# A hybrid decoder trunk on one core: where the second block's mixer is placed among the expert retrieval of the first

## The chip, the cores and the metric

The kernel runs on one core of a Trainium2 chip. The metric is the device time of one execution in microseconds (us). Engines: PE (TensorE), DVE (VectorE), ACT (ScalarE), POOL (GpSimd) and SP (SyncE, which only issues DMAs here). The 16 DMA engines of the core move everything between HBM and SBUF.

## What is computed

Input x is 256 tokens of 1024 float32 values. Two layers follow, each a mixer and an expert retrieval (PEER), both added to the residual stream, and a final RMSNorm. Cut to its core:

```python
for layer in range(2):
    hn = rms_norm(h, norm1_g[layer])
    proj = hn @ w_in[layer]                      # 1024 -> 2824
    o_a = gdn_mixer(...)        # gated delta rule, 4 heads, with a triangular inverse
    o_b = s5_mixer(...)         # diagonal state space scan, 16 groups x 64 states
    o_c = diff_attn_mixer(...)  # causal differential attention, 4 heads
    h = h + concat([o_a, o_b, o_c]) @ w_out[layer]
    h = h + peer_ffn(rms_norm(h, norm2_g[layer]), ...)

def peer_ffn(x, wq, keys, u_tab, v_tab):         # for each token and each of 8 heads
    # two top-16 of 128 sub-keys, top-16 of their 256 sums: 16 experts of 16384
    gate = softmax(top_s)
    act = gelu(einsum('bthkd,btd->bthk', u_tab[expert], xt))
    return einsum('bthk,bthkd->btd', gate * act, v_tab[expert])
```

Each token needs 8 x 16 rows of u_tab and as many of v_tab, of 4 KB each.

## The kernel before

**Blocks, pairs, slots.** A block is 128 tokens in one layer; there are four, numbered i = 0 to 3 (layer i // 2, token half t = i % 2). PEER of a block takes its 8 heads in 4 pairs, and a pair of heads has 32 slots. In a slot one row of u_tab per partition is gathered (128 x 1024, 0.524 MB), DVE forms its dot product with the token (`dot`, L1699), and one row of v_tab is gathered, which PE later weighs and sums over the partitions (`values`). All 16 pairs, n = 0 to 15, run as one chain of 512 dots. A selection `top(n + 1)` (L1610 to L1683) runs on DVE in small parts among the dots of pair n; it yields the indices of the next pair's gathers.

**The mixer of the next block rides along.** Block 0's mixer runs alone at the start (`first_mixer`). While the four pairs of block b are worked off (128 slots), every engine also works off the mixer of block b + 1, cut in steps. PE, DVE and ACT each have their own generators `mix(i)` and `attention(i)`, which yield the slot at which the next step is due; after slot j of pair n the engine calls `stages.advance(PAIR * (n % 4) + j)`, which runs all steps whose due slot is not above that number. The numbers are written out by hand (34, 36, 38, 44.6, ... 121), and `place(i, slot)` (L111) turns them into slots: as they are for blocks 2 and 3, and by a straight line for block 1, because block 1 has no tables to make (these are slots 1 to 28 of blocks with t = 0) and so can use the slots that these take elsewhere. A due slot sets the order within an engine's program; what is waited for is semaphores alone.

**Steps spoken of here**, by their written number s. DVE: norm1 (the reciprocal of the root, L1424) at 34; log decay at 42 and 44.3; the four S5 parts `ssm(i, j)` (L1375 to L1392) at 44.6, 48.9, 54 and 59; `silu` (L1593) at 51.5 and 53.2; the lower triangle at 62.3; S5 output at 65 and 66.3; GLU at 68.2; masks (L1588) at 59.6 + 3 lv; attention maximum (L1399) at 69.8; attention scales and differences to 75.2; residual (L1518) at 99; second norm (L1521, L1524) at 100; `top(4 * i)` from 109 to 118.1; gates at 121. ACT: the square and root of the second norm (`norm_square`, L2077 and L2079) at 99.5. PE: turning the normed input at 36, the weight fills from 38 on.

**Weights.** A mixer reads 39 chunks of 0.524 MB (`CHUNKS`: u, qkv, z, v, q, k, two halves each, glu, the output projection, PEER's wq), which SP loads into a ring of 4 (`wring`), one each time PE has used one. Block 1's first six chunks are loaded ahead, into v buffers 5 to 10.

**Rings and the order on GpSimd.** Gathers are issued by GpSimd from one in-order program: for each slot j of pair n the u gather (it waits until the dot 7 rows before is done, since `uring` has 7 buffers), then as many v gathers as `v_goal(n, j)` asks for. In pair 0 v starts at slot 11 and takes every second slot, until all 11 buffers of `vring` are asked for. v gather q, counted from 0, waits for these things:

```python
            elif q >= VRING:
                pool.wait_ge(v_used.sem, q - VRING + 1)
            elif q >= FREE_SLOT:                                # FREE_SLOT = 5
                pool.wait_ge(*chunk_done(1, q - FREE_SLOT + 1))
            elif q == 0:
                pool.wait_ge(*chunk_done(0, NC))
```

PE sums the rows of pair n in pair n + 1, four rows at a time, in slots 1, 5, ... 29, once DVE has written their weights (`weights(n)`, after the first dot of pair n + 1).

**ACT within a pair.** In slot 24 ACT makes the softmax of the next pair; in slot 31, ahead of the mixer's steps due there, it waits for the pair's gelu argument from DVE:

```python
                if j == PAIR - 1:
                    act.wait_ge(gelu_arg.sem, n + 1)
                    S.activation(gt, gt, ACT.Tanh, scale=GELU).then_inc(gelu_tanh.sem, 1)
                stages.advance(PAIR * (n % 4) + j)
```

DVE's slot 31 is: dot, `gelu(n)` (which signals the argument), then the mixer's steps due.

Of the kernel before, what the change touches and what calls it, by code (L numbers as in the profile page):

```python
# [110 lines left out]

def place(i, slot):

    return slot if i != 1 else 2 + (slot - 32) * 117.0 / 88.0


class Stages:
# [19 lines left out]
def _build(nc, ctx, x, w_blocks, cols_d, rows_d, keys_d, u_tab, v_tab, cst_d, fin_d, out):  # L137
# [419 lines left out]
    def _(pe):  # L557
# [358 lines left out]
        def mix(i):  # L916
            t, layer = i % 2, i // 2
            yield place(i, 36)
            pe.wait_ge(*hn1_ready(i, 1))
            if i == 1:  # L920
                pe.wait_ge(s0_ready.sem, 5)
            else:
                pe.wait_ge(*sc_ready(i, 0))
            turn_mix((M0, M1))
            yield place(i, 38)
            pe.wait_ge(*trT_ready(i, 1))
            fill(i, "u", 0, M2, True)
            yield place(i, 39)
            pe.wait_ge(*trT_ready(i, 2))
            fill(i, "u", 1, M2, True)  # L930
# [1718 lines left out]
```

## Time and profile before

| | |
|---|---|
| median of 3 runs | 1603.93 us (1601.36 to 1607.55) |
| profiled execution | 1604.18 us, its span 1602.2 us |
| DVE, POOL, PE busy | 1110.2, 987.0, 967.3 us |
| ACT busy | 292.0 us |
| moved by DMA | 628.66 MB, mean 392 GB/s |
| of it by gathers (POOL's queue) | 536.94 MB |
| of it by SP's queue | 90.53 MB |

The span counts from the first to the last instruction. The page cuts it in 40 slices of 40 us; in those from 280 us on the DMA engines move 407 to 420 GB/s, but for three (385, 354 and the last, 307). The times of the four pairs of block 0, by the first dot of each in the trace, are 146.7, 215.8, 305.8 and 392.8 us, and block 1's pairs begin at 489.2 us.

### The profile page before, as it was taken

What the parts mean: (1) busy time and instruction counts of PE and PEld (TensorE: products, weight loads), DVE (VectorE), ACT (ScalarE), POOL (GpSimd) and SP (SyncE); (2) the same over time, 40 slices, a digit from 0 to 9 for tenths busy, and PEclk for the clock granted to TensorE, in tenths of its full rate; (3) what the DMA queues carried; (4) which work ended last, traced back from release to release, by engine and by line L of the source; (5) the groups of instructions that cost most, each with busy time, mean ns of one, the idle gap of its engine ahead of it and who ended that gap; (6) DMA issues with size and microseconds to landing.
All of it is one profiled execution on the core that took longest, in us unless ns stands there. A gap on an engine that the chain in (4) does not pass through costs nothing.

```text
span 1602.2 us, 18901 instructions
## 1 busy us (share of the span) xinstructions
PE 967.3 (60%) x5966; PEld 565.9 (35%) x5966; DVE 1110.2 (69%) x2868; ACT 292.0 (18%) x830; POOL 987.0 (62%) x1031
## 2 busy tenths in 40 slices
PE   9986796865634357887554347977674334333335
PEld 8875674532400036654330024844350000000001
DVE  5948999775657987777466766779557767676440
ACT  5343421411000032332110014314110000000000
POOL 0003656777666676657657775646757777777773
PEclk9998898977866579999776568989886555555567
DMA  9527999999999999999999999999999999999997
GB/s 373 200 91 255 384 371 419 407 419 419 418 420 420 417 385 419 418 419 419 419 419 420 419 420 418 418 416 354 419 420 419 419 419 420 419 419 419 420 418 307
DMA packets 172899, 628.66 MB, mean 392 GB/s; under 512 B 19200, under 2 KB 19200, under 8 KB 172800
## 3 DMA queue, kind: packets, MB, share of 16 engines
q0 software_dynamic: 147456, 536.94, 82.8%
q1 hardware_dynamic: 25344, 90.53, 14.4%
q8 instruction: 47, 0.77, 0.2%
q14 instruction: 52, 0.43, 0.1%
HBM read 626.34 MB, written 1.05 MB: 392 GB/s over the span
## 4 chain that ended last, share of the span: by engine, by line
DMA 28%; DVE 24%; POOL 17%; issue 14%; PE 12%; DVEq 4%; ACT 1%; POOLq 0%; SPq 0%; ACTq 0%
DMA uring<-in_u_tab,small 19%; PE ps L559 12%; DVE uring L1699 10%; POOL uring L2505 7%; POOL vring L2505 6%; DMA vring<-in_v_tab,small 4%; DMA wring<-in_v_tab,small 1%; DMA gd<-in_u_tab,small 1%; POOL gd L2505 1%; POOL wring L2505 1%; DMA uring<-in_v_tab,small 1%; DMA rows<-in_rows 1%; DVE sel L1659 1%; DVE small L1636 1%; DVE sel L1663 1%
## 5 line engine op out<-in xcount | busy, mean ns | idle before, releaser
L1699 DVE CUSTOM_DVE_ANT_0 uring<-uring,ps 128x1024 f32<-128x1024 f32 x462 | 558.3, 1217 | 282.8 <-DMA uring<-in_u_tab,small 262.9
L2505 POOL DMA_INDIRECT uring<-in_u_tab,small x462 | 446.3, 966 | 405.4 <-DVE small L1699 136.6
L559 PE MATMUL ps<-vring,wmat 128*32 128x512 f32 x1748 | 328.3, 874 | 397.4 <-DMA vring<-in_v_tab,small 343.9
L2505 POOL DMA_INDIRECT vring<-in_v_tab,small x437 | 419.9, 961 | 151.1 <-issue 115.6
L559 PEld LDWEIGHTS ps<-vring,wmat 128*32 128x32 f32 x1748 | 58.7, 138 | 587.9 <-DMA vring<-in_v_tab,small 396.4
L559 PE MATMUL ps<-hnT,wring 128*128 128x128 f32 x1200 | 151.5, 283 | 1.7 <-ACT hn L2013 1.2
L559 PEld LDWEIGHTS ps<-hnT,wring 128*128 128x128 f32 x1200 | 142.3, 196 | 25.6 <-issue 20.6
L559 PE MATMUL ps<-wring,hnT 128*128 128x256 f32 x344 | 84.4, 396 | 1.8 <-ACT hnT L2013 1.5
L2495 ACT ACTIVATE small<-small 128x32 f32<-128x32 f32 x16 | 3.7, 230 | 442.5 <-DVEq L1708 442.5
L559 PE MATMUL ps<-gd 128*128 128x128 f32 (+1 forms) x508 | 70.4, 289 | 15.4 <-ACT gd L2013 13.5
L559 PEld LDWEIGHTS ps<-gd 128*128 128x128 f32 x508 | 63.6, 196 | 31.7 <-ACT gd L2013 17.6
L2013 ACT ACTIVATE gd<-ps 128x512 f32<-128x512 f32 (+2 forms) x79 | 43.2, 548 | 165.7 <-PE ps L559 145.4
L559 PEld LDWEIGHTS ps<-wring,hnT 128*128 128x128 f32 x344 | 65.8, 199 | 21.4 <-issue 10.0
L1699 DVE CUSTOM_DVE_ANT_0 gd<-gd,ps 128x1024 f32<-128x1024 f32 x40 | 48.8, 1220 | 33.4 <-DMA gd<-in_u_tab,small 33.2
L559 PE MATMUL ps<-phase_c,wmat 128*32 128x512 f32 x28 | 25.0, 1048 | 43.6 <-DMA vbuf<-in_v_tab,small 43.6
L2288 ACT ACTIVATE small<-small 128x16 f32<-128x16 f32 x32 | 6.6, 209 | 230.1 <-DVE small L1647 229.9
L559 PE MATMUL ps<-kT,wmat 128*32 128x512 f32 x28 | 23.6, 994 | 40.9 <-DMA vring<-in_v_tab,small 34.0
L559 PE MATMUL ps<-wring,wmat 128*32 128x512 f32 x112 | 23.6, 987 | 37.5 <-DMA wring<-in_v_tab,small 30.4
L2505 POOL DMA_INDIRECT gd<-in_u_tab,small x40 | 37.5, 937 | 12.2 <-issue 11.6
L559 PE MATMUL ps<-cst 128*128 128x512 f32 x76 | 41.9, 640 | 2.4 <-ACTq L2051 1.7
L1699 DVE DVE_READ_ACCUMULATOR2_ANT small<- 128x1 f32 x512 | 42.4, 83 | 0.0
L559 PE MATMUL ps<-sa,cz 128*32 128x128 f32 x224 | 31.7, 308 | 4.4 <-DVEq L1393 4.4
(434 smaller groups left out, 1501.7 us busy)
## 6 DMA issues: line engine op xcount, KB each, us to landing
wring<-in_w_blocks SPq DMA_DIRECT2D x120, 512.0 KB, 7.2
vring<-in_w_blocks SPq DMA_DIRECT2D x32, 512.0 KB, 9.4
uring<-in_u_tab,small POOLq DMA_INDIRECT x462, 12.3
vring<-in_v_tab,small POOLq DMA_INDIRECT x437
wring<-in_cols SPq DMA_DIRECT2D x3, 512.0 KB, 6.9
sa<-in_rows SPq DMA_DIRECT2D x3, 512.0 KB, 6.5
h<-in_x SPq DMA_DIRECT2D x2, 512.0 KB, 8.9
keysT<-in_keys SPq DMA_DIRECT2D x2, 512.0 KB, 13.2
```

The lines of the kernel that those rows point to most:

```text
L559: return nc.tensor.matmul(o, a, b, start=start, stop=True, skip_group_check=True)
L1636: V.max_index(tp[:, hd, 0:8], tv[:, hd, 0:8], cand1[:, hd, :])
L1659: V.tensor_tensor(oh.rearrange("p g k n -> p (g k) n"), bc(ab_f[:, pc][:, :, None], [P, 32 * nh, TOPK]), bc(iota[:, None, :], [P, 32 * nh, ...
L1663: V.tensor_tensor(oh, oh, bc(sif[:, pc].rearrange("p (g n) -> p g n", n=TOPK)[:, :, None, :], [P, 2 * nh, TOPK, TOPK]), ALU.mult)
L1699: V.tensor_tensor_reduce(row_, row_, xp, 1.0, 0.0, ALU.mult, ALU.add, dots[:, j:j + 1]).then_inc(dot_done.sem, 1)
L2013: return S.activation(dst, src, ACT.Copy, scale=scale)
L2288: S.activation(gate[:, hd, :], gate[:, hd, :], ACT.Exp, accum_out=gz[:, hd:hd + 1])
L2495: S.activation(gt, gt, ACT.Tanh, scale=GELU).then_inc(gelu_tanh.sem, 1)
L2505: nc.gpsimd.indirect_dma_start(dst, None, table, bass.IndirectOffsetOnAxis(ap=index, axis=0)).then_inc(done.sem, 16)
```

## The change

One line: the straight line by which block 1's written numbers become slots.

```diff
 def place(i, slot):
 
-    return slot if i != 1 else 2 + (slot - 32) * 117.0 / 88.0
+    return slot if i != 1 else 10 + (slot - 32) * 110.0 / 88.0
```

Number 32 maps to slot 10 in place of slot 2, number 120 to slot 120 in place of 119. It holds for PE, DVE and ACT alike; SP's and GpSimd's programs don't call `place`. No instruction and no transfer is added or taken away, and blocks 0, 2 and 3 are placed as before.

## Rows read from the trace of the kernel before

**Rows 1.** The page: busy time of the engines, and landing times of the gathers.

```profile
...
PE 967.3 (60%) x5966; PEld 565.9 (35%) x5966; DVE 1110.2 (69%) x2868; ACT 292.0 (18%) x830; POOL 987.0 (62%) x1031
...
uring<-in_u_tab,small POOLq DMA_INDIRECT x462, 12.3
...
```

**Rows 2.** Stretches of the span: busy us per engine, PE clock, DMA share, GB/s.

```profile
...
138.00:172.00 34.00, 19.47 (x156) 18.33 (x157) 32.13 (x106) 15.95 (x44) 23.18 (x25) 0.80 0.93 335
172.00:200.00 28.00, 17.83 (x101) 14.93 (x101) 26.11 (x64) 10.54 (x28) 15.78 (x16) 0.80 1.00 389
200.00:235.00 35.00, 33.80 (x250) 27.98 (x249) 32.03 (x82) 10.93 (x40) 18.77 (x19) 0.97 0.97 364
235.00:280.00 45.00, 32.80 (x215) 21.47 (x214) 41.91 (x98) 7.93 (x14) 29.41 (x30) 0.89 1.02 418
280.00:305.00 25.00, 22.95 (x138) 12.72 (x137) 19.58 (x44) 10.75 (x32) 17.33 (x19) 1.00 1.01 402
305.00:550.00 245.00, 122.82 (x676) 57.35 (x680) 169.14 (x487) 24.35 (x66) 167.89 (x177) 0.72 1.03 419
...
```

**Rows 3.** Waits of DVE, 305 to 550 us: total us, times, longest.

```profile
...
DVE uring L1699 <- DMA uring<-in_u_tab,small: 59.8, 41, 3.8
...
```

**Rows 4.** DVE in order of time: start, us, instruction, idle before it.

```profile
...
155.85 0.15 DVE L1424 RECIPROCAL small<-small 128x1 f32<-128x1 f32 x1
...
172.36 1.20 DVE L1699 CUSTOM_DVE_ANT_0 uring<-uring,ps 128x1024 f32<-128x1024 f32 x1
...
215.78 1.21 DVE L1699 CUSTOM_DVE_ANT_0 uring<-uring,ps 128x1024 f32<-128x1024 f32 x1
...
```

**Rows 5.** DVE by line, 198 to 216 us: count, busy us and mean ns, idle before.

```profile
...
L1385 DVE TENSOR_TENSOR_SCAN sa<-small,sa 128x128 f32<-128x128 f32 x4 | 1.6, 466 | 0.1
L1593 DVE SCALAR_TENSOR_TENSOR keyT<-keyT,ps 128x512 f32<-128x512 f32 (+1 forms) x2 | 1.1, 553 | 0.1
L1375 DVE TENSOR_TENSOR sa<-sa,phase_c 128x512 f32<-128x512 f32 x1 | 0.7, 693 | 1.1 <-PE ps L559 1.1
...
L1378 DVE TENSOR_TENSOR sa<-sa 128x256 f32<-128x256 f32 x1 | 0.4, 426 | 0.1
...
```

**Rows 6.** DVE in order of time, at the attention's maximum.

```profile
...
282.58 1.29 DVE L1399 TENSOR_REDUCE small<-ps 128x2 f32<-128x512 f32 x2 [2.03 <-PE ps L559]
...
```

**Rows 7.** GpSimd in order of time: v gathers 5, 10 and 11.

```profile
...
175.62 0.98 POOL L2505 DMA_INDIRECT vring<-in_v_tab,small  x1 [0.31 <-issue]
...
201.26 0.94 POOL L2505 DMA_INDIRECT vring<-in_v_tab,small  x1 [0.30 <-issue]
...
223.27 0.94 POOL L2505 DMA_INDIRECT vring<-in_v_tab,small  x1 [0.30 <-issue]
...
```

**Rows 8.** PE in order of time: the turned input, chunks 1 and 2, 7 and 8.

```profile
...
157.24 1.97 PE L562 MATMUL ps<-cst,hn 128*128 128x128 f32 x8 [13.65 <-ACT hn L2013]
159.61 4.63 PE L559 MATMUL ps<-hnT,vring 128*128 128x128 f32 x32 [0.40 <-ACTq L2106]
...
175.48 3.84 PE L559 MATMUL ps<-hnT,wring 128*128 128x128 f32 x32
...
```

**Rows 9.** DMA issues, 150 to 200 us: count, median us to landing.

```profile
...
uring<-in_u_tab,small POOLq DMA_INDIRECT x23, 6.0
...
```

**Rows 10.** DVE in order of time, at block 1's second norm.

```profile
...
385.64 0.16 DVE L1521 RECIPROCAL small<-small 128x1 f32<-128x1 f32 x1 [0.31 <-ACT small L2079]
385.89 1.28 DVE L1524 SCALAR_TENSOR_TENSOR hn<-h,small,sa 128x1024 f32<-128x1024 f32 x1
...
```

**Rows 11.** ACT in order of time, at block 1's second norm.

```profile
...
382.81 1.06 ACT L2077 ACTIVATE hn<-h 128x1024 f32<-128x1024 f32 x1 [39.06 <-DVE h L1518]
...
384.02 1.28 ACT L2079 ACT_TABLE_LOAD   x1
385.31 0.29 ACT L2079 ACTIVATE small<-small 128x1 f32<-128x1 f32 x1
...
```

## The prediction

> **What bounds the kernel now.** I read the slices of the page first, for the course of the transfers, then the stretches of the trace around block 1's mixer, then who waits for whom, then single instructions. The vector engine is busy for 69% of the span, GpSimd for 62% [rows 1]: neither fills it. The bound is what the 16 DMA engines move. From 305 to 550 us they move 419 GB/s without a break [rows 2], and there the dot products (DVE L1699) stand 59.8 us idle waiting for their gathered rows [rows 3]. At 419 GB/s a gather of 0.524 MB takes 1.25 us, and the vector engine needs 1.2 us for a dot; a slot (one dot, one u row, one v row) costs 2.5 us of transfer, more where weights are loaded. So an engine's saving counts only where the DMA engines move less than 419 GB/s.
>
> Around this change they do so here [rows 2]: 172 to 200 us 389 GB/s, which is 28 x 30/419 = 2.0 us lost; 200 to 235 us 364 GB/s, 4.6 us; 235 to 280 us 418 GB/s, 0.1 us; 280 to 305 us 402 GB/s, 1.0 us. From 138 to 172 us 335 GB/s are moved, but this is the start of pair 0, ahead of every step that the change can touch except one reciprocal. What can be won is thus at most 2.0 + 4.6 + 0.1 + 1.0 = 7.7 us, and only as far as the cause of the loss is the mixer's vector work. That the vector engine is the cause is seen in its busy time in these stretches, 26.1 of 28 us and 32.0 of 35 us [rows 2].
>
> **What moves, and when.** A step of block 1 with number s was due at slot 2 + 1.330(s-32) and is due at slot 10 + 1.25(s-32). The first vector step, s = 34, goes from 4.7 to 12.5; s = 54 from 31.3 to 37.5; s = 70 from 52.5 to 57.5; s = 100 from 92.4 to 95; the last, s = 121, from 120.3 to 121.3. Nothing is added or removed: no instruction, no byte. Block 1 still hands over within pair 3, and the selection for pair 4 ends at s = 118.1, slot 117.6 for 116.5; GpSimd wants those indices when dot 122 (of 128) is done, so that costs nothing as long as the lead of 4 slots isn't used up. Blocks 2 and 3 keep their slots. Whatever block 1 gains or loses by slot 128 carries to the end unchanged.
>
> **Pair 0, vector engine.** norm1's reciprocal ran at 155.85 us; it will run after dot 13, ahead of dot 14, which starts at 172.36 us [rows 4]. All chunks of weights follow from it, as PE's slots in pair 0 have nothing else in them. Of the vector work, the steps with s between 48 and 54 leave pair 0: one S5 part whole (a scan group 1.6 us, four operations of 0.7, two of 0.4) and both silu products (1.1 us): 1.6 + 4 x 0.7 + 2 x 0.4 + 1.1 = 6.3 us [rows 5]. Slot 32 should come some 6 us earlier than at present. This is no gain in itself: the weights of s 49 to 54 (v0 second half, v1, q0 first half, four chunks of 0.524 MB) aren't loaded in pair 0 any more either, 4 x 1.25 = 5.0 us of transfer that must be made up in pair 1. By the DMA engines the account of pair 0 is +6.3 - 5.0 = 1.3 us to the good.
>
> **Pair 1.** There the same 6.3 us come back to the vector engine, and work of the end of the pair leaves it. At slot 54 the old map has passed the GLU product, a mask of 0.7 us (128x512, as the 0.7 us of rows 5) and the attention maximum, 1.3 us after an idle wait of 2.0 us on PE [rows 6]; with 1.3 us for the small ones beside them (an estimate, from the 0.4 us of rows 5) that is 5.3 us which the new map does later. So the vector engine would allow slot 54 to come 5.3 us earlier. The DMA engines don't: 235 to 280 us is full, and by slot 54 both maps have asked for the same weights but the chunk "glu" (1.25 us). So the gain at slot 54 is the loss that is avoided before 235 us, between 0 and 5.3 us.
>
> **How much loss is avoided.** 172 to 200 us: GpSimd issues gathers back to back where nothing holds it (0.94 us and 0.3 us of gap, 1.24 us each), which by itself fills the DMA engines. It was held by the ring of u rows, i.e. by dots that were late because of the mixer's work. Without that work most of the 2.0 us go, less a new wait (next part): +0.7 us taken. 200 to 235 us: v gather 10, the last of the first eleven, is issued at 201.3 us and the next not before 223.3 us [rows 7], since all 11 v buffers are full until pair 1's first sums have read them. In these 22 us only u rows and weights are moved. The change shortens this hole: the last v gather goes out near 197 us (from 178.4 us on, next part, 5 v and 10 u gathers at 1.24 us, 18.6 us), and slot 32, after which the hole ends, comes about 6 to 8 us earlier than its 215.8 us [rows 4]; the hole keeps some 17 to 19 of its 22 us. A fifth of 4.6 us is 0.9 us, and the lower weight traffic in it takes part of that back, while the closer spacing of the chunks in pair 1 gives some: +1.3 us in all for the two stretches from 200 us on is my choice, nearer the 0 end because the hole's cause (full v ring, slow slots) stays. Sum: 0.7 + 1.3 = 2.0 us, bounds 0 and 5.3 us.
>
> **The new wait on GpSimd's queue.** v gathers 5 to 10 write the buffers that hold block 1's first six chunks, so each waits for its chunk; behind it in GpSimd's queue wait the u gathers, and for those the dots. Before, v gather 5 went out at 175.62 us [rows 7]. PE turned the input at 157.24 us, began chunk 1 at 159.61 us (two chunks in 4.63 us, so the first ended near 161.9 us, 6.1 us after norm1), and began chunk 7 at 175.48 us, 19.6 us after norm1 [rows 8]. With norm1 at 172.3 us, chunk 1 ends near 178.4 us and chunk 6 before 191.9 us. v gather 5 waits 178.4 - 175.6 = 2.8 us; gather 10, at 201.3 us before and 197 us after, doesn't. The dots don't starve: they are 7 rows behind. The DMA engines have less than 2.8 us of queued work (a gather lands 6.0 us after its issue here [rows 9], against 12.3 us over the whole span [rows 1]), so I count 1.3 us of the 2.8 as lost, already taken off in the +0.7 above.
>
> **Slot 95.** ACT executes its step s = 99.5 in slot 92 now; it falls to 94.4, so to slot 95, the last of pair 2, where ACT first waits for that slot's gelu argument. The vector engine's s = 100 falls to exactly 95.0, the same slot, and needs ACT's result. Before, ACT began its square at 382.81 us, when the sum was there, and took until 385.6 us; a whole dot lay between and the vector engine waited 0.31 us [rows 10, 11]. Now it waits the full 2.8 us and a tanh, about 3.1 us, with the weights for the next pair's v sums queued behind it on its own engine, then PE's sums and, through the v buffers, GpSimd. The cover is the queue of the DMA engines: landing takes 12.3 us there instead of 6.0 us, so 6 us of work stand in it. I cost it at 0, and at 2.8 us if the cover fails. What the trace shows for ACT is a table load of 1.28 us with the square root right behind it, 2.8 us from the square's start to the root's end [rows 11]. The Trainium skill (ScalarE: Activation LUTs, What ACT_TABLE_LOAD costs) adds a drain of about 1.38 us to each switch of the table set, 2.66 us in all; by that the wait would be 4.2 us in place of 2.8 us. The row shows no such second part, and even 4.2 us lie under the cover, so the forecast would be the same.
>
> **The rivals.** (a) Nothing moves: the holes are set by the full v ring, and the slots' order inside them is immaterial. The 0.7 and 1.3 us are then 0: 1604.2 us, give or take 1. For it: DMA engines full from 235 us on; against it: the vector engine's busy share before. (b) The vector engine is the only bound until slot 54 and all its 5.3 us count: 1604.2 - 5.3 = 1598.9 us. Against it: 418 GB/s from 235 to 280 us. (c) Slower: slot 95. If the u and v rings don't refill the DMA queue after the stall (GpSimd's 1.24 us per gather is no faster than the engines' 1.25 us, so a queue once drained stays short), the 3.1 us and the 1.5 us of reciprocal and scaling behind it [rows 10] reach the transfers. It decides from the point where the stall exceeds the roughly 6 us of queued transfers; then the price is 2.8 to 4.6 us, and with none of the gain 1607.0 to 1608.8 us. (d) Slower: GpSimd's wait for chunk 1. If chunks 1 to 6 come at the pace of a slower PE clock, each v gather waits anew; one wait of 2.8 us fully lost and nothing won gives 1607.0 us.
>
> **How the numbers follow.** The profiled execution took 1604.18 us, 0.25 us from the median of 1603.93 us, so I predict against 1604.2: 1604.2 - 2.0 = 1602.2 us. Chances: forecast (1600.5 to 1603.2) 0.43, (a) 0.22, (b) 0.12, (c) 0.12, (d) 0.08, anything else 0.03. The range takes in (a) and (b) whole and (c) and (d) for the most part: 1597.5 to 1608.0 us. A measurement of this kernel can't tell less than 0.5%, 8 us, from no change. The whole loss that can be won is 7.7 us, so faster by over 8 us has 0.04; slower by over 8 us needs (c) and (d) together or an unseen one, 0.05; within 0.5% 0.91.
>
> **What would show it.** After: norm1 near 172.3 us, PE idle before it for some 30 us where it was 13.65 [rows 8]; a wait of GpSimd on PE of some 3 us near 176 us; slot 32 near 209 us, 6 to 7 us earlier than 215.8; higher GB/s from 178 to 200 us; a gain that shrinks to 2 us by slot 56; a wait of DVE on ACT of about 3 us at the reciprocal before pair 3, with 419 GB/s kept. I am wrong if slot 56 comes over 4 us earlier or later than now, or if the rate dips near 385 us.

## The result, and the profile after

The changed kernel takes 1608.88 us (median of 19 runs, 1604.65 to 1613.66) and the kernel before 1605.52 us (19 runs, 1601.36 to 1608.21). The ratio is 1.0022, interval 1.0015 to 1.0029: 3.4 us slower, where 2.0 us faster was forecast. It is less than half a per cent, as expected, but outside the range and on the wrong side. The prediction held that this kernel's times can't tell less than 0.5% from no change; with 19 runs of each the interval is 0.07% wide to either side, so 0.2% can be told. The profiled execution took 1606.48 us, with a span of 1604.5 us against 1602.2 us.

The stretches of the changed kernel come first (columns as in [rows 2]: length, busy us of PE, PEld, DVE, ACT, POOL, PE clock, DMA share, GB/s).

```profile
138.00:172.00 34.00, 6.42 (x59) 5.73 (x58) 32.02 (x108) 6.96 (x15) 22.29 (x24) 0.66 0.87 314
172.00:200.00 28.00, 22.31 (x161) 21.36 (x162) 25.51 (x67) 17.90 (x51) 17.25 (x19) 0.80 0.90 342
200.00:235.00 35.00, 31.86 (x211) 25.37 (x211) 30.48 (x77) 5.71 (x16) 19.90 (x20) 0.95 0.99 385
235.00:280.00 45.00, 34.44 (x267) 25.53 (x266) 42.44 (x97) 11.67 (x38) 27.81 (x28) 0.89 1.03 419
280.00:305.00 25.00, 21.21 (x105) 12.29 (x104) 17.44 (x38) 7.23 (x22) 17.18 (x18) 1.00 1.03 419
305.00:330.00 25.00, 21.73 (x151) 14.46 (x150) 21.02 (x62) 13.17 (x36) 17.36 (x18) 0.93 1.00 395
330.00:550.00 220.00, 108.62 (x592) 47.08 (x590) 150.73 (x431) 18.19 (x47) 147.50 (x156) 0.68 1.03 419
```

Against [rows 2], 172 to 200 us fell from 389 to 342 GB/s, 200 to 235 us rose from 364 to 385, 280 to 305 us rose from 402 to 419, and a new dip stands at 305 to 330 us. In lost transfer (length times the share missing to 419 GB/s, as in the prediction) that is 2.0 to 5.1 us, 4.6 to 2.8, 1.0 to 0, and 0 to 1.4: a balance of 9.3 us against 7.6, so 1.7 us worse. The row from 138 to 172 us is worse too (314 for 335 GB/s), but this is a later start: the first dot stands at 148.44 us here and at 146.65 us before. Of the kernels below with the new line in pair 0, e6, e7 and e8 have it at 146.4 to 146.6 us and e15b at 149.3 us, and e10, with the old steps there, at 148.3 us. So it isn't the change's doing, and 1.8 of the 2.3 us between the two spans are no evidence of anything. The medians are.

The worst place is found by GpSimd in order of time, with the turned input and the first chunks on PE:

```profile
174.09 0.14 DVE L1424 RECIPROCAL small<-small 128x1 f32<-128x1 f32 x1
175.47 1.97 PE L562 MATMUL ps<-cst,hn 128*128 128x128 f32 x8 [30.10 <-ACT hn L2013]
177.84 4.71 PE L559 MATMUL ps<-hnT,vring 128*128 128x128 f32 x32 [0.40 <-ACTq L2106]
...
176.17 0.94 POOL L2505 DMA_INDIRECT uring<-in_u_tab,small  x1 [1.36 <-DVE small L1699]
181.57 0.94 POOL L2505 DMA_INDIRECT vring<-in_v_tab,small  x1 [4.47 <-PE ps L559]
182.82 0.94 POOL L2505 DMA_INDIRECT uring<-in_u_tab,small  x1 [0.30 <-PE ps L559]
```

v gather 5 waits 4.47 us for chunk 1, and all of GpSimd's queue with it. The transfers themselves, from 172 to 200 us in 40 slices of 0.7 us, show what follows, with GpSimd's queue under them:

```profile
GB/s 398 415 392 404 404 410 410 421 416 421 416 386 105 0 0 0 129 310 345 281 339 410 339 310 281 345 339 339 363 380 410 410 421 416 427 416 421 421 439 392
...
q0 software_dynamic: 2619, 9.54, 89.3%
```

Three slices are at 0 (181.1 to 183.2 us) and one on either side near 100: the DMA engines ran empty. The other thing to see is the queue that is absent. Of 9.58 MB, 9.54 are GpSimd's gathers (q0) and the rest is instructions; SP's weight loads (q1) have no row. The first line below is SP's in the kernel before (three loads from 177.56 us, the next at 193.33 us), the second is the changed kernel's, where the first load comes at 198.50 us:

```profile
177.56 3.84 SPq L539 DMA_DIRECT2D wring<-in_w_blocks  x3
...
198.50 0.33 SPq L539 DMA_DIRECT2D wring<-in_w_blocks  x1
```

Each of these loads waits for an earlier chunk to be used, so they are late because the front (norm1 to chunk 6) is late.

Further on, VectorE waits for the attention's scores and for ScalarE's root, and the rate dips only behind the first, from 310 to 330 us. Just ahead of that dip GpSimd stands for 2.52 us, where in the kernel before it stands at most 0.63 us at a time between 288 and 330 us (the three lines are DVE, POOL, DVE; behind them are the stretches around the root):

```profile
296.09 1.29 DVE L1399 TENSOR_REDUCE small<-ps 128x2 f32<-128x512 f32 x2 [4.76 <-PE ps L559]
...
308.63 0.94 POOL L2505 DMA_INDIRECT vring<-in_v_tab,small  x1 [2.52 <-DVE small L1699]
...
397.42 0.16 DVE L1521 RECIPROCAL small<-small 128x1 f32<-128x1 f32 x1 [3.01 <-ACT small L2079]
```
```profile
385.00:390.00 5.00, 5.00 (x24) 1.92 (x24) 1.23 (x2) 0.00 (x0) 2.48 (x3) 0.71 1.03 419
390.00:395.00 5.00, 0.21 (x1) 0.00 (x0) 4.08 (x8) 0.53 (x2) 3.59 (x5) 0.97 1.02 419
395.00:400.00 5.00, 0.00 (x0) 0.00 (x0) 2.50 (x3) 2.31 (x4) 1.43 (x2) 0.50 1.03 419
```

### The profile page after: what moved, and what is told of

The parts are those of the page before. It is cut to its first block, busy times and chain, and to the rows that moved or that the text cites. A ratio compares the mean times of both kernels' runs of the same rounds, so it can differ in the third digit from the quotient of the medians.

```text
span 1604.5 us, 18901 instructions
## 1 busy us (share of the span) xinstructions
PE 965.4 (60%) x5966; PEld 565.4 (35%) x5966; DVE 1110.3 (69%) x2868; ACT 291.8 (18%) x830; POOL 984.2 (61%) x1031
## 4 chain that ended last, share of the span: by engine, by line
DMA 30%; DVE 23%; POOL 15%; PE 14%; issue 12%; DVEq 4%; ACT 2%; POOLq 0%; ACTq 0%; SPq 0%
DMA uring<-in_u_tab,small 20%; PE ps L559 14%; DVE uring L1699 10%; DMA vring<-in_v_tab,small 6%; POOL vring L2505 6%; POOL uring L2505 5%; POOL gd L2505 1%; DMA wring<-in_v_tab,small 1%; DMA uring<-in_v_tab,small 1%; POOL wring L2505 1%; DMA sa<-in_u_tab,small 1%; DMA rows<-in_rows 1%; DVE sel L1659 1%; DVE small L1625 1%; DVE small L1636 0%
## 6 DMA issues: line engine op xcount, KB each, us to landing
vring<-in_w_blocks SPq DMA_DIRECT2D x32, 512.0 KB, 10.1
```

## The experiments

Theory at the start: GpSimd's stop behind v gather 5 is dearer than costed, and later work pays too. Rivals: slot 95; the later steps alone. All edits below are to the changed kernel or to the one before, as said. "Lost" is transfer lost in us by the formula above, from each kernel's own stretches; differences are ratio times 1605.6 us (for the changed kernel 3.4 us by the medians, 3.5 by the ratio). The ratios are those on record; they aren't quotients of the medians, and differ from these by up to 0.1%.

| kernel | 172–200 | 200–235 | 280–305 | 305–330 | lost, sum | measured, us against before |
|---|---|---|---|---|---|---|
| before | 2.0 | 4.6 | 1.0 | 0 | 7.6 | 0 |
| e13b wait alone | 3.4 | 2.4 | 0.1 | 0 | 5.9 | +0.8 (-0.6 to 2.2) |
| e10 attention alone | 2.2 | 3.7 | 1.7 | 0.7 | 8.3 | 0.0 (-1.4 to 1.4) |
| e12 front 5 slots later | 2.6 | 6.1 | 0 | 0.1 | 8.8 | +1.9 (0.5 to 3.4) |
| changed | 5.1 | 2.8 | 0 | 1.4 | 9.3 | +3.4 (2.4 to 4.7) |
| e7 v gathers later | 4.2 | 1.7 | 1.0 | 3.2 | 10.1 | +1.8 (0.2 to 3.5) |
| e5 front on the old line | 1.1 | 6.7 | 0 | 2.4 | 10.2 | +1.4 (-0.2 to 3.2) |
| e14b e5, VectorE's attention later | 1.1 | 6.8 | 0 | 3.0 | 10.9 | +5.5 (3.4 to 7.5) |
| e6 only the front moved | 6.6 | 3.6 | 1.6 | 0.2 | 12.0 | +4.8 (2.9 to 6.7) |
| e11 line between | 1.6 | 5.3 | 5.0 | 0.7 | 12.6 | +3.7 (2.2 to 5.1) |
| e15b e7 and e14b together | 4.2 | 1.1 | 0.1 | 8.3 | 13.7 | +6.4 (3.9 to 8.8) |
| e8 second norm apart | 6.7 | 3.5 | 0.1 | 3.6 | 13.9 | +2.6 (1.1 to 4.0) |
| e9 attention earlier | 1.2 | 6.8 | 3.7 | 5.7 | 17.4 | +8.3 (6.1 to 10.4) |

The order of the last two columns is roughly the same: the time goes with the transfer lost before 330 us, but single cells are loose. e8 differs from the changed kernel only from slot 93 on, so the two should lose the same before 330 us, and their profiles read 13.9 and 9.3 us. Part of this is where the pair begins. With 138 to 172 us counted in (and 235 to 280 us), and each sum held against the span of the same profile, the agreement is better: 14.5 us lost and a span of 1602.2 us before, 16.4 and 1604.6 in e10, 17.8 and 1604.5 in the changed kernel, 18.6 and 1605.9 in e6, 19.8 and 1607.2 in e8, 23.3 and 1610.1 in e9. Over all thirteen the span's difference to the kernel before is within 2.3 us of the loss's, for nine of the other twelve within 1.0 us.

**A first session told nothing (e1 to e4).** These are e5 to e8 on another session, in which the kernel before took 1776.05 us and moved less than 419 GB/s where nothing held it (last section). The ratios were 1.0004 (0.9961 to 1.0046), 1.0043 (1.0003 to 1.0083), 0.9970 (0.9922 to 1.0017) and 0.9986 (0.9948 to 1.0025). With intervals of 1% they decide nothing, except that only the front moved (e2) is not faster.

> The changed kernel, but block 1's steps up to number 43.5 (norm, turned input, chunks 1 to 6, first S5 inputs) keep their old slots; only the later steps are placed by the new line. Theory A (the time was lost because GpSimd's v gather 5 waited 4.47 us for chunk 1 and the DMA engines ran dry from 180 to 190 us): the wait is gone, 180 to 190 us moves 380 GB/s or more in place of 136 and 324, and the kernel is 3 to 6 us faster than the changed one, i.e. 0 to 2 us faster than the kernel before (ratio 0.998 to 1.000). Rival B (the later steps' places cost the time: the attention at the end of pair 1 and the second norm in slot 95): the kernel stays 3 us slower than before (ratio 1.002).

> The complement: steps up to 43.5 by the new line, all later steps in their old slots (those already due run at once). Theory A: GpSimd's wait of 4 to 5 us is there, and the kernel is 3 to 5 us slower than before (ratio 1.002 to 1.003), as slow as the changed kernel or slower, since nothing of the vector work of pair 0 is moved out of it. Rival B: as fast as before (ratio 1.000), wait or not.

> The changed kernel, with v gathers 5 to 10 asked for in slots 25 to 30 of pair 0 in place of 21 to 31 by twos, so that u gathers are not behind the wait for chunk 1. Theory A1 (the loss is the in-order queue: u gathers stuck behind v gather 5): u gathers flow, most of the loss is won back, ratio 0.999 to 1.0005. Theory A2 (the loss is lack of work: with v, and the weights, held back until PE has run, the u ring alone can't fill the DMA engines): under 330 GB/s from 178 to 188 us remains, half or less is won back, ratio 1.001 to 1.002. Rival B: no effect, 1.002.

> The changed kernel with block 1's steps 99 and 99.5 0.75 slot earlier, so that ACT does the second norm's square in slot 94, ahead of the gelu of pair 2, and the vector engine meets it one slot later. Theory A: the wait of DVE on ACT (3.0 us) falls under 1 us and the time stays that of the changed kernel (ratio 1.002). Rival B: 2 to 3 us are won back (ratio 1.000 to 1.001).

**The front: e5 and e6.** e5 is the changed kernel with norm1 to chunk 6 on the old line; e6 has the front on the new line and the rest on the old.

```
 def place(i, slot):
+    if i == 1 and slot <= 43.5:          # e5; e6 has "slot > 43.5"
+        return 2 + (slot - 32) * 117.0 / 88.0
     return slot if i != 1 else 10 + (slot - 32) * 110.0 / 88.0
```

> The kernel of e1_front_early once more, since the chip of that session moved 300 to 419 GB/s in steady stretches and its spread of 1% covers the effect. Theory A (GpSimd's wait for chunk 1): no such wait, 180 to 190 us at 380 GB/s or more, ratio 0.998 to 1.000. Rival B (places of the later steps): ratio 1.002.

> The kernel of e2_front_late_only once more on a quiet chip. Theory A: wait of 4 to 5 us on GpSimd, ratio 1.002 to 1.004. Rival B: ratio 1.000.

e5 took 1605.91 us, ratio 1.0009 (0.9999 to 1.0020); e6 1609.52 us, 1.0030 (1.0018 to 1.0042). A front moved alone is thus slower for certain, by as much as the changed kernel within the intervals; taken back, 2.0 of the 3.4 us go, and what is left can't be told from nothing. e6 isn't the wait alone, though. Its v gather 5 waits 5.04 us, and as the later steps keep their old places and crowd behind the late front (VectorE begins no dot between 189.28 and 202.07 us), GpSimd stands a second time, for 6.19 us:

```profile
180.07 0.94 POOL L2507 DMA_INDIRECT vring<-in_v_tab,small  x1 [5.04 <-DVE small L1701]
...
204.11 0.94 POOL L2507 DMA_INDIRECT uring<-in_u_tab,small  x1 [6.19 <-PE ps L561]
```

In e5 the wait of GpSimd is gone and 172 to 200 us carry 403 GB/s, but the next stretch loses what it won:

```profile
172.00:200.00 28.00, 11.70 (x78) 9.86 (x77) 25.11 (x62) 9.37 (x23) 19.43 (x20) 0.75 1.02 403
200.00:235.00 35.00, 31.63 (x200) 25.29 (x199) 29.94 (x75) 5.98 (x23) 17.91 (x18) 0.86 0.90 339
```

**The gathers at the wait: e7.** All steps stay on the new line; v gathers 5 to 10 get later places among the u gathers.

```
             if n == 0:
+                if j >= 21:
+                    return 5 if j < 25 else min(VRING, j - 19)
                 return max(0, (j + 1 - (PAIR - 2 * VRING)) // 2)
```

> The kernel of e3_v_later once more. A1 (in-order queue): ratio 0.999 to 1.0005. A2 (lack of work for the DMA engines until PE has run): under 330 GB/s from 178 to 188 us stays, ratio 1.001 to 1.002. Rival B: 1.002.

1606.00 us, ratio 1.0011 (1.0001 to 1.0022). v gather 5 goes out at 183.51 us without a wait for PE, and 1.8 of the 3.4 us go. But 172 to 200 us still lose 4.2 us, against 2.0 before:

```profile
178.00:188.00 10.00, 10.00 (x84) 9.76 (x82) 9.57 (x17) 4.88 (x18) 7.06 (x7) 0.94 0.83 268
```

This is what the expectation called lack of work (under 330 GB/s, ratio 1.001 to 1.002). GpSimd stands no longer than 1.76 us at a time here, yet the v gathers come later and SP's loads only at 196.50 us, and the u gathers, which wait for dots, don't fill the engines. So the order on GpSimd's queue isn't the whole of the loss.

Pair 1's first dot stands where the prediction wanted it:

```profile
146.58 1.22 DVE L1699 CUSTOM_DVE_ANT_0 uring<-uring,ps 128x1024 f32<-128x1024 f32 x1 [0.23 <-issue]
...
209.28 1.22 DVE L1699 CUSTOM_DVE_ANT_0 uring<-uring,ps 128x1024 f32<-128x1024 f32 x1 [0.56 <-DMA uring<-in_u_tab,small]
```

Counted from the first dot that is 62.7 us. Before it is 215.78 - 146.65 = 69.1 us, in the changed kernel 213.93 - 148.44 = 65.5 us. So the 6.4 us of vector work that leave pair 0 are real, and the kernel is nevertheless not faster.

**Slot 95: e8.** The residual on VectorE (number 99) and the square and root on ScalarE (99.5) come 0.6 numbers, or 0.75 slots, earlier, the latter into slot 94; VectorE's own step of the second norm (100) stays in slot 95.

```
 def place(i, slot):
+    if i == 1 and slot in (99, 99.5):
+        slot -= 0.6
```

> The kernel of e4_norm2_apart once more. Theory A: the wait of DVE on ACT falls under 1 us, ratio 1.002 as for the changed kernel. Rival B: ratio 1.000 to 1.001.

1608.30 us, ratio 1.0016 (1.0007 to 1.0025). The wait for the root is down to 0.83 us and the kernel stays as slow within the intervals (+2.6, 1.1 to 4.0, for +3.4):

```profile
397.10 0.16 DVE L1523 RECIPROCAL small<-small 128x1 f32<-128x1 f32 x1 [0.83 <-ACT small L2081]
```

**Is it the wait? e13b.** The kernel before with one edit: v gathers 5 to 10 wait for the ninth signal of block 1's chunks. No step moves.

```
-                pool.wait_ge(*chunk_done(1, q - FREE_SLOT + 1))
+                pool.wait_ge(*chunk_done(1, max(9, q - FREE_SLOT + 1)))
```

> The kernel before, with one edit: the v gathers 5 to 10 wait for the eighth or ninth chunk's worth of TensorE's work, so that GpSimd stops at v gather 5 some 5 us (it stopped 4.47 us there in the changed kernel), while no step of block 1 is moved. Theory A (the stop of GpSimd's one queue is what the changed kernel pays for): GpSimd shows a wait for PE of 3 to 6 us near 176 us, the rate at 180-190 us falls under 330 GB/s, the loss of transfer at 172-200 us rises from 2.0 us to 4.5-7, and the kernel is 2 to 4 us slower, a ratio of 1.0012 to 1.0025. Theory B (the stop costs nothing by itself; the losses come from where the later steps fall): the transfers come back later and the ratio is under 1.0006.

> e13 again, since the chip moved 300 to 419 GB/s in its stretches and the intervals were 1% wide; its wait was 14.2 us there, too long, because the chunks of block 1 ran 12 us later than in the profile of before. In a session at 419 GB/s GpSimd should stop at v gather 5 from 175.6 to about 181 us. Theory A (this stop alone costs): rate at 180-190 us under 330 GB/s, loss of transfer at 172-200 us from 2.0 to 4.5-7 us, ratio 1.0012 to 1.0025. Theory B (the stop costs nothing by itself): ratio under 1.0006.

The first try (e13) fell into a session like that of e1: ratio 1.0157 (1.0076 to 1.0239), with a wait of 14.2 us, since block 1's chunks came 12 us later there; it tests a far longer wait. e13b is the test: 1605.65 us, ratio 1.0005 (0.9996 to 1.0014). This is a miss for my theory, and the most useful run of the study. The stop is longer than in the changed kernel:

```profile
181.40 0.94 POOL L2505 DMA_INDIRECT vring<-in_v_tab,small  x1 [6.41 <-PE ps L559]
```

yet the engines never stand still. The same view as above, 172 to 200 us in slices of 0.7 us:

```profile
GB/s 404 421 398 445 398 421 363 386 298 269 298 228 181 287 275 328 316 246 351 258 380 375 363 398 398 386 392 421 421 415 427 410 433 398 427 410 433 410 433 398
...
q0 software_dynamic: 2243, 8.17, 74.6%
q1 hardware_dynamic: 576, 2.10, 22.1%
```

2.10 MB came by SP's queue, issued while GpSimd stood:

```profile
177.10 3.84 SPq L539 DMA_DIRECT2D wring<-in_w_blocks  x3
```

Three loads of 1.25 us each lie in the hole (SP issued them from 177.1 to 180.9 us). The 1.4 us that are still lost by 200 us (3.4 for 2.0) come back by 235 us (2.4 for 4.6). The expectation for a costly stop (4.5 to 7 us lost, ratio from 1.0012) isn't met, that for a free one (under 1.0006) is, though the interval leaves room for up to 2.2 us. So this stop of GpSimd was nearly free, with SP's loads beside it. In the changed kernel the chunk that releases v gather 5 also stands ahead of all that release weight loads, so both queues are silent at once.

**A front half way: e12 and e11.** e12 is the kernel before with the front at 7 + (s-32) x 1.25; e11 puts all of block 1 on a line between the two.

```
+    if i == 1 and slot <= 43.5:                                    # e12
+        return 7 + (slot - 32) * 110.0 / 88.0
+    return slot if i != 1 else 6 + (slot - 32) * 113.5 / 88.0      # e11
```

> The kernel before, with the steps up to 43.5 alone later, norm1 after dot 10 (in place of 5; 13 in e6). Theory A with its threshold: chunk 1 ends near 173 us, ahead of the 177 us at which GpSimd asks for it, no wait over 0.5 us, ratio 0.9995 to 1.0007 where e6 had 1.003. Without a threshold: about half to two thirds of e6, 1.0015 to 1.002.

> One line for all steps, 6 + (s - 32) * 113.5/88: norm1 after dot 9, scores in slot 54, the last attention step in slot 62. Theories A and C: chunk 1 is done by 173 us, so GpSimd doesn't wait for it, and the attention ends ahead of the border, so most of both losses are gone: ratio 0.9985 to 1.0003. If the loss grew evenly with the start (no threshold), the ratio would be half of the changed kernel's, 1.001.

e12 took 1607.03 us, ratio 1.0012 (1.0003 to 1.0021), e11 1608.90 us, 1.0023 (1.0014 to 1.0032). In neither does v gather 5 wait for PE; e12 loses at 200 to 235 us instead (6.1 us), and its 1.0012 lies between the two expectations (up to 1.0007 if only the wait costs, from 1.0015 if the delay does), so a later front may cost something without the wait. e11, for which I had expected at most 1.0003, is a miss: it loses 5.0 us at 280 to 305 us, where VectorE stops 6.23 us for the scores. In that stop GpSimd's u gathers, which wait for dots, stop too (first VectorE's row, then the stretches):

```profile
292.15 1.29 DVE L1399 TENSOR_REDUCE small<-ps 128x2 f32<-128x512 f32 x2 [6.23 <-PE ps L559]
```
```profile
290.00:295.00 5.00, 5.00 (x27) 1.94 (x27) 2.61 (x6) 1.24 (x5) 0.56 (x1) 1.00 0.91 374
295.00:300.00 5.00, 5.00 (x22) 2.67 (x20) 3.89 (x11) 2.19 (x7) 3.19 (x4) 1.00 0.50 148
```

POOL is busy 0.56 of 5 us and the rate falls to 148 GB/s right behind: the same picture as at 180 us, with another reason for the stop.

**The attention: e9, e10, e14, e15.** e10 is the kernel before with the attention's steps 4.7 slots later on all engines; e9 is e5 with them 1.5 slots earlier; e14b is e5 with VectorE's steps 69.8 to 75.2 alone 1.2 slots later; e15b is e7 with the same.

```
+def place_attention(i, slot):          # + 4.7 in e10, - 1.5 in e9
+    return place(i, slot) + 4.7 if i == 1 else place(i, slot)
-            yield place(i, 69.8)       # and the like; in e14 and e15
+            yield later_slot(i, 69.8)  # VectorE's alone, + 1.2
```

> The kernel before, with block 1's attention steps alone 4.7 slots later, about where the changed kernel has them. Theory C: 1 to 2.5 us are lost between 290 and 330 us, ratio 1.0007 to 1.0015, with no wait of GpSimd near 177 us. Rival D: ratio 1.000.

> The kernel of e5_front_early (old slots up to number 43.5, new line behind), with block 1's attention steps 1.5 slots earlier on PE, DVE and ACT, so that the first scores (69) fall to slot 55 in place of 57, where PE first does four rows of sums, and the last ones ahead of slot 63. Theory C (the second loss is the attention, placed at the border of pairs 1 and 2): 305 to 330 us moves 410 GB/s or more in place of 379, the wait of DVE for the first attention maximum falls from 4.8 to 3 us or less, ratio 0.998 to 1.0000. Rival D (the dense later line as a whole, or the emptier slots 24 to 32): the loss stays, ratio 1.001.

> The changed kernel with the steps to slot 43.5 on the line of before (as in e5, 1.0009) and VectorE's steps of the attention (69.8 to 75.2) 1.2 slots later, so that VectorE comes to the maxima after TensorE's scores are done. Theory A (the rest of the 1.4 us that e5 has over the kernel before is VectorE waiting for scores in its order): the wait of the attention's maximum for PE falls from 4.8 us to under 2.5, 305-330 us carries over 405 GB/s, ratio 0.998 to 1.000. Theory B (the loss sits at 200-235 us, where e5 has 339 GB/s, and this edit touches nothing there): the wait falls, but the ratio stays at 1.0005 to 1.0015.

> The changed kernel with the two costs taken away at their places, all of its steps left on the new line: v gathers 5 to 10 in later slots of pair 0 (as in e7, 1.0011), and VectorE's steps of the attention 1.2 slots later. Theory A (the wait of GpSimd and the wait of VectorE for scores are the whole loss, and the vector work moved out of pair 0 is then a gain): 172-200 us over 350 GB/s, 305-330 us over 405 GB/s, ratio 0.997 to 0.9995. Theory B (what is won in pair 0 is lost elsewhere whatever is mended): ratio 1.0000 to 1.0012.

> e14 again for the same reason. Theory A (the remaining 1.4 us of e5 is VectorE waiting for scores in its order): the wait of the attention's maximum for TensorE falls from 4.8 us to under 2.5, 305-330 us over 405 GB/s, ratio 0.998 to 1.000. Theory B (it sits at 200-235 us, or the wait only changes its place): ratio 1.0005 to 1.0015. In the first try 305-330 us carried only 244 GB/s with a wait of VectorE for ScalarE of 11.3 us, which speaks for B with the wait turned into one of the softmax behind it.

> e15 again for the same reason. Theory A (GpSimd's wait and VectorE's wait for scores are the whole loss): 172-200 us over 350 GB/s, 305-330 us over 405 GB/s, ratio 0.997 to 0.9995. Theory B (what is won in pair 0 is lost elsewhere, or the attention's wait changes its place): ratio 1.0000 to 1.0025; the first try had 252 GB/s at 305-330 us, which speaks for B.

e10: 1606.26 us, ratio 1.0000 (0.9991 to 1.0009), although its wait for the scores is as long as in the changed kernel:

```profile
294.31 1.29 DVE L1404 TENSOR_REDUCE small<-ps 128x2 f32<-128x512 f32 x2 [4.78 <-PE ps L564]
```

So neither a later attention nor one wait of 4.8 us costs anything that the times can tell (1.4 us to either side). e9: 1613.74 us, 1.0052 (1.0038 to 1.0065), expected 0.998 to 1.000: a miss, with two waits of 3.5 us for scores. e14 and e15 ran first in the poor session (1.0059, 1.0007 to 1.0111, and 1.0047, 0.9996 to 1.0098), then as e14b: 1609.51 us, 1.0034 (1.0021 to 1.0047), and e15b: 1610.62 us, 1.0040 (1.0024 to 1.0055). Both are misses for "VectorE's wait for scores is the rest". e14b shortened that wait only from 4.75 to 3.62 us, and VectorE now waits twice as long (2.5 us in e5) for the root by which ScalarE scales the attention's output:

```profile
295.64 1.29 DVE L1406 TENSOR_REDUCE small<-ps 128x2 f32<-128x512 f32 x2 [3.62 <-PE ps L566]
...
328.46 0.18 DVE L1587 RECIPROCAL small<-small 128x4 f32<-128x4 f32 x1 [4.90 <-ACT small L2286]
```

In e15b both maxima wait (4.07 and 4.94 us), GpSimd stands for 10.21 us, and 305 to 330 us carry only 280 GB/s (310 to 315 us: 10 GB/s). The 4.6 us more than in e7 (1.0040 for 1.0011) are in this stretch (8.3 us lost for 3.2):

```profile
313.54 0.94 POOL L2510 DMA_INDIRECT vring<-in_v_tab,small  x1 [10.21 <-DVE small L1704]
```

The waits move from one step to the next; in these two kernels, shifting VectorE's steps alone was worse than leaving them with the others'.

None of these kernels beats the one before. e13b, e10 and e5 can't be told from it.

## Why the prediction was wrong

**The bound** held. From 330 to 550 us the changed kernel moves 419 GB/s too, and the times of all kernels roughly follow the transfer lost before 330 us (table).

**Pair 0, vector engine.** norm1 was forecast at 172.3 us, right ahead of dot 14; it stands at 174.09 us ahead of the dot at 174.15, the same place with the start 1.8 us later. PE idled 30.10 us before it (some 30 forecast, 13.65 before, [rows 8]). The 6.3 us of [rows 5] gave 6.4 us where nothing else intervened (e7), 3.6 us in the changed kernel. The mechanism and the size were right.

**The step that failed: the term of +0.7 us for 172 to 200 us.** It was to leave 1.3 us of the 2.0 us lost there, with 1.3 us of GpSimd's new wait of 2.8 us counted as lost and the rest as covered by queued transfers. The stretch lost 5.1 us: 3.1 us worse than before in place of 0.7 us better. Behind this stands the account of pair 0, which set 6.3 us of vector work against 5.0 us of weight loads and took loads as a burden only. In the kernel before, three of SP's loads keep the DMA engines busy from 177.56 us on. They hang on the front's chunks, and with the front 18 us later they come 21 us later, so they are missing just where GpSimd stands. I didn't ask which transfers would be left during the stop. e13b, with a stop of 6.41 us and the loads beside it, costs +0.8 us (-0.6 to 2.2); e6, with one of 5.04 us and no loads, 4.8 us (2.9 to 6.7), of which its second stop has an unknown share.

**The wait's length** was mis-sized too: forecast 2.8 us, measured 4.47 us. I halved the 4.63 us of two chunks [rows 8]. But the granted clock was 0.50 (the level of 1.2 GHz) until the first of the two was under way, so that one takes more than half, and GpSimd's gather started 181.57 - 174.09 = 7.5 us after norm1, not 6.1. This isn't an effect of the longer idle time of PE. The clock stands at 0.50 ahead of these chunks in the kernel before too, and the two take 4.63 us there and 4.71 us here:

```profile
155.00:160.00 5.00, 2.36 (x10) 1.96 (x11) 4.83 (x20) 2.66 (x7) 3.63 (x4) 0.50 0.97 365
160.00:165.00 5.00, 5.00 (x41) 5.00 (x41) 4.91 (x17) 0.78 (x4) 3.23 (x5) 0.87 1.01 390
```

The queue, once empty, refilled slowly: GpSimd issues a gather every 1.24 us, about as fast as the engines move one, and from 184 to 192 us the slices stand at 281 to 410 GB/s.

**200 us on.** Forecast +1.3 us; the stretches 200 to 235 and 280 to 305 us give +1.8 + 1.0 = 2.8 us. But 305 to 330 us lose 1.4 us where nothing was lost before. The v hole, forecast 17 to 19 us, is 21.5 us (gathers at 200.26 and 221.80 us). e13b has the same better rate at 200 to 235 us (390 GB/s) with no vector work moved. So that gain may be mostly the earlier loss coming back, and can't be credited to the change.

**Slot 56.** The gain was to shrink to 2 us there and to stay. Counted from the first dot, slot 56 came at 285.96 - 148.44 = 137.5 us for 287.76 - 146.65 = 141.1 (3.6 us early, within the 4 us that I had set as a limit). Slot 64 then came at 162.1 us (310.55) for 159.1 (305.76), 3.0 us late. The attention's maxima have gone from the slots before and after 56 to behind it, and the first now waits 4.76 us for PE where it waited 2.03 [rows 6]. The prediction moved its 5.3 us of work but didn't ask whether PE's scores would still be ready. In the changed kernel they stand behind the v sums and the level products of that slot:

```profile
288.12 1.92 PE L559 MATMUL ps<-vring,wmat 128*32 128x512 f32 x16
289.97 2.05 PE L559 MATMUL ps<-gd 128*128 128x128 f32 x16
291.86 1.02 PE L559 MATMUL ps<-cst 128*128 128x512 f32 x2
292.81 1.13 PE L559 MATMUL ps<-kT,hn 64*128 64x256 f32 x4
```

**Slot 95** was right. The wait is 3.01 us (3.1 forecast), the rate stays at 419 GB/s, and e8 takes it away without a clear gain. The square starts at 394.60 us and the reciprocal at 397.42 us, 2.8 us as in [rows 11]. The Trainium skill (ScalarE: Activation LUTs, What ACT_TABLE_LOAD costs) puts a drain of 1.38 us on each switch; this trace has again the load of 1.28 us and the root at its end (395.79, 397.09 us), with no room for it between them.

**The rivals.** (a) and (b) are out, (c) is out by e8 and by the rate. (c)'s price of up to 1608.8 us is nearest to the measured 1608.88 us, but by luck, as nothing was lost at its place. (d) named the right place (1607.0 us), but its mechanism, one wait fully lost, doesn't hold as put: e13b has a longer wait at no price that can be told. By the traces it needs the missing weight loads.

**What stays open.** That the missing weight loads are what makes the stop dear is argued, from the two queues' bytes, from e13b and from the low rate that stays in e7; but in e13b VectorE's work of pair 0 stays too, and a moved front with its loads left in place wasn't run. That a later front costs time is shown by e6, whose interval is clear of nothing. Its share in the changed kernel is less sure: 2.0 us by e5 and 1.8 us by e7, each with some 2 us to either side, an estimate from the intervals of the two kernels compared, so that neither is clear of nothing by itself. The remaining 1.4 to 1.8 us go by the traces with the dip at 305 to 330 us, for which the prediction had no term, but e5's remainder (-0.2 to 3.2) could be nothing, and my attempts to take that dip away (e9, e14b, e15b) made it larger. Which alignment of the attention's steps, the sums and the selections makes it small isn't settled; e10 has the same first wait at no loss of time.

## What to carry to other kernels

Before work is moved out of a stretch, list for each queue what it would have put into the transfers there. A wait on an in-order issuing queue was nearly free here while another queue had work in those microseconds, and moving the producer silenced both. Where steps on several engines hand over to each other slot by slot, a saving on one engine can end at the next hand-over (3.6 us at slot 56, gone by slot 64), so work out for the first steps behind it whether their producer still comes first. And a loss made good further on can show as a gain there: sum over the stretches before crediting one.

## What the runs showed of the hardware

Two of the five sessions of experiments gave 1776.05 and 1788.21 us for the kernel before, 11% over the others' 1605.6. The transfers were the difference; why they were slower isn't known. In that of e1, stretches that stand at 419 GB/s in the kernel before read (305 to 550 us, 700 to 850 us):

```profile
305.00:550.00 245.00, 136.10 (x741) 74.82 (x739) 147.89 (x389) 35.05 (x92) 150.54 (x158) 0.74 0.97 377
700.00:850.00 150.00, 94.98 (x591) 64.28 (x590) 95.82 (x226) 35.88 (x115) 77.92 (x81) 0.78 0.87 335
```

Within a session the intervals were 1% wide there, so differences of some us could only be read in the other sessions.

The first dot comes at 146.2 to 149.3 us in profiles of kernels that are alike up to there. Two spans of one profile each can thus differ by 3 us for no reason in the edit.

TensorE's first chunk in pair 0 began at the lower level. In the changed kernel the granted clock was 0.50 from 150 to 178 us, with PE idle from 145.4 to 175.5 us, and 1.00 (2.4 GHz) from 180 us. In the kernel before it was 0.50 from 150 to 160 us, with PE idle for 13.65 us, and 1.00 from 162 us. In both, single matmuls of the first two chunks took up to 0.58 us, with a median of 0.275 us.
